# Expert rows one at a time instead of in pairs, with other constants in the planner that places them among a two-layer block's matmuls

## The reference

```python
g = jax.nn.softmax(top, axis=-1).astype(xs.dtype)
a = jax.nn.gelu(jnp.einsum('nd,nhjd->nhj', xs, u[eid]), approximate=False)
return jnp.einsum('nhj,nhjd->nd', g * a, v[eid])
```

## Time and profile before

| | us |
|---|---|
| median of 3 runs (lowest, highest) | 3435.36 (3432.03, 3439.66) |
| profiled execution, its own time | 3441.62 |
| span of its trace | 3439.5 |
| TensorE busy, 82% of the span | 2810.3 |
| DVE busy | 1919.4 |
| ScalarE busy | 1111.6 |

### The profile page before, as it was taken

The page is one execution under the profiler, slowest core; times in us unless marked ns, Lnnn a source line. Parts: engine busy times, 40 slices in busy tenths (PEclk is TensorE's granted clock), DMA queues, the critical chain, the costliest instruction groups (busy, mean ns, idle before and its releaser), DMA issues.

```text
span 3439.5 us, 40717 instructions
## 1 busy us (share of the span) xinstructions
PE 2810.3 (82%) x15162; PEld 1750.6 (51%) x15162; DVE 1919.4 (56%) x4582; ACT 1111.6 (32%) x3213; POOL 853.5 (25%) x772
## 2 busy tenths in 40 slices
PE   8999998989888999888775555699999986655555
PEld 6777887655545666564431111278788841211111
DVE  4564764566676556456676766422300256666665
ACT  2232002343574455323533232232310123323222
POOL 0000001234332333223344444200000034444443
PEclk9999999999999999999898776899999987776776
DMA  8264764989998999879999999733144299999998
GB/s 327 99 208 148 289 239 169 369 339 373 373 358 329 417 421 420 336 299 371 404 372 420 415 412 412 308 111 110 57 152 151 73 376 414 411 419 403 411 415 335
DMA packets 151780, 1071.76 MB, mean 312 GB/s; under 512 B 16668, under 2 KB 19356, under 8 KB 23200
## 3 DMA queue, kind: packets, MB, share of 16 engines
q0 software_dynamic: 110592, 805.36, 57.8%
q1 hardware_dynamic: 40992, 263.82, 20.5%
HBM read 1068.06 MB, written 1.05 MB: 311 GB/s over the span
## 4 chain that ended last, share of the span: by engine, by line
PE 51%; DMA 26%; DVE 12%; ACT 6%; issue 3%; POOL 2%; SPq 0%; DVEq 0%; POOLq 0%; ACTq 0%
PE bank L438 38%; DMA ring<-in_experts,eid 25%; PE bank L452 11%; DVE ring L1494 5%; POOL ring L1968 2%; ACT topk_work L1007 1%; ACT topk_work L1000 1%; DMA ring<-in_quads 1%; ACT topk_work L997 1%; ACT L997 1%; DVE state L1729 1%; PE bank L465 1%; PE bank L687 0%; DVE topk_work L1464 0%; PE bank L568 0%
## 5 line engine op out<-in xcount | busy, mean ns | idle before, releaser
L1968 POOL DMA_INDIRECT ring<-in_experts,eid x768 | 853.3, 1111 | 2563.2 <-PE bank L452 1284.2
L452 PE MATMUL bank<-ring,topk_work 64*64 64x512 f32 x6144 | 975.0, 763 | 557.6 <-ACT topk_work L1007 544.3
L1494 DVE CUSTOM_DVE_ANT_0 ring<-ring,h2tok 128x1024 f32<-128x1024 f32 x768 | 937.4, 1225 | 589.1 <-DMA ring<-in_experts,eid 574.9
L452 PEld LDWEIGHTS bank<-ring,topk_work 64*64 64x64 f32 x6144 | 234.7, 158 | 1185.5 <-ACT topk_work L1007 878.3
L997 ACT ACTIVATE topk_work<-topk_work 128x2 f32<-128x2 f32 x384 | 78.0, 203 | 1139.9 <-DVE topk_work L1494 1132.6
L438 PE MATMUL bank<-h_even,weights 128*128 128x256 f32 (+1 forms) x1280 | 293.2, 388 | 4.4 <-ACT h_even L1080 4.0
L438 PEld LDWEIGHTS bank<-h_even,weights 128*128 128x128 f32 (+1 forms) x1280 | 240.9, 190 | 60.8 <-issue 22.8
L438 PE MATMUL bank<-h_odd,weights 128*128 128x256 f32 (+1 forms) x1008 | 228.3, 382 | 0.0
L1007 ACT ACTIVATE topk_work<-const,topk_work 128x64 f32<-128x64 f32 x768 | 225.6, 341 | 0.2 <-ACT topk_work L1000 0.2
L438 PEld LDWEIGHTS bank<-h_odd,weights 128*128 128x128 f32 (+1 forms) x1008 | 187.5, 189 | 49.9 <-issue 23.8
L1000 ACT ACTIVATE topk_work<-topk_work 128x1 f32<-128x1 f32 x768 | 184.6, 287 | 12.6
(11 more groups left out here) (252 smaller groups left out, 3243.6 us busy)
## 6 DMA issues: line engine op xcount, KB each, us to landing
weights<-in_quads SPq DMA_DIRECT2D x151, 1024.0 KB
ring<-in_quads SPq DMA_DIRECT2D x84, 1024.0 KB, 4.9
ring<-in_experts,eid POOLq DMA_INDIRECT x768
weights<-in_quads SPq DMA_DIRECT2D x6, 768.0 KB
ring<-in_quads SPq DMA_DIRECT2D x6, 768.0 KB, 4.5
weights<-in_quads SPq DMA_DIRECT2D x12, 256.0 KB
xT<-in_xT SPq DMA_DIRECT2D x2, 1024.0 KB, 11.7
out<-state SPq DMA_DIRECT2D x4, 256.0 KB, 5.3
```

The source lines that it names most:

```text
L452: x = nc.tensor.matmul(acc[g][out, :], diag[mine, J % 4, :], ring[mine, J % RING, D + h * 512:D + (h + 1) * 512], start=first, stop=J % TI ...
L1494: v.tensor_tensor_reduce(row, row, h2tok[:, u // UNITS % 2, :], 1.0, 0.0, ALU.mult, ALU.add, dots[:, u % 2, j:j + 1]).then_inc(S["dot_done ...
L1968: pool.indirect_dma_start(ring[:, J % RING, :], None, d["experts"], bass.IndirectOffsetOnAxis(eid[:, u % 2, j:j + 1], 0)).then_inc(gathere ...
```

## The change

Pairs become single rows on TensorE, ScalarE and DVE; counters and marks that counted pairs count rows. ScalarE has a Gelu of one column for each row, 384 more instructions in all. In the planner LAG falls from 5.0 to 4.0, and modelled time is added after each unit of the softmax attention (UNIT_TAKES 2.0), after each of the two gate blocks (GATES_TAKE 5.0) and after the turn of a tile's sums (SUM_TAKES 2.0); `breathe` with a hole looks half of it ahead as before.

```diff
@@ -52,22 +52,22 @@
 UNITS = PH
 TILE_ROWS = UNITS * PTOP
 GROUP_ROWS = 2 * TILE_ROWS
-GROUP_PAIRS = GROUP_ROWS // 2
-TILE_PAIRS = TILE_ROWS // 2
-UNIT_PAIRS = PTOP // 2
 RING = 6
 BANKS = 6
 FIXED, EXTRA = 3, 4
 
 
-PER_LOAD, LANDS, LAG = 2.5, 2.0, 5.0
+PER_LOAD, LANDS, LAG = 2.5, 2.0, 4.0
 LEAD_CHOICE = 10.0
+
+
+UNIT_TAKES, GATES_TAKE, SUM_TAKES = 2.0, 5.0, 2.0
 
 
 BESIDE, PACE = 0.1, 1.0
 DIAG_LAG = 3.0
 
-TURN_FROM, TURN_EVERY, TURN_LAG = 24, 4, 2
+TURN_FROM, TURN_EVERY, TURN_LAG = 48, 8, 4
 
 
 class Count:
...
@@ -437,22 +437,22 @@
                 plan.now += size * 4 / 2400.0
                 return nc.tensor.matmul(out, lhsT, rhs, start=first, stop=last, **kw)
 
-            def row_pair(n):
-                for J in (2 * n, 2 * n + 1):
-                    k, first = J // TILE_ROWS, J % TILE_ROWS == 0
-                    if first and J:
-                        for g in range(2):
-                            pe.wait_ge(*at("evicted", "acc", k - 1, g))
-
-                    pe.wait_ge(S["diag_ready"], J + 1)
-                    for h in range(2):
-                        out = slice(h * BLK, (h + 1) * BLK)
-                        for g in range(2):
-                            mine = slice(g * BLK, (g + 1) * BLK)
-                            x = nc.tensor.matmul(acc[g][out, :], diag[mine, J % 4, :],
-                                                 ring[mine, J % RING, D + h * 512:D + (h + 1) * 512],
-                                                 start=first, stop=J % TILE_ROWS == TILE_ROWS - 1, skip_group_check=True)
-                    x.then_inc(S["row_used"], 1)
+            def row(J):
+
+                k, first = J // TILE_ROWS, J % TILE_ROWS == 0
+                if first and J:
+                    for g in range(2):
+                        pe.wait_ge(*at("evicted", "acc", k - 1, g))
+
+                pe.wait_ge(S["diag_ready"], J + 1)
+                for h in range(2):
+                    out = slice(h * BLK, (h + 1) * BLK)
+                    for g in range(2):
+                        mine = slice(g * BLK, (g + 1) * BLK)
+                        x = nc.tensor.matmul(acc[g][out, :], diag[mine, J % 4, :],
+                                             ring[mine, J % RING, D + h * 512:D + (h + 1) * 512],
+                                             start=first, stop=J % TILE_ROWS == TILE_ROWS - 1, skip_group_check=True)
+                x.then_inc(S["row_used"], 1)
 
             def tile_sum(k):
 
@@ -465,22 +465,22 @@
                             x = nc.tensor.matmul(b[:, c * P + h * BLK:c * P + (h + 1) * BLK],
                                                  sums(k, h)[:, c * P:(c + 1) * P], ident[:, g * BLK:(g + 1) * BLK],
                                                  start=True, stop=True)
+                    plan.now += SUM_TAKES
                     full(x, "yt", k, g)
 
-            def emit(n):
-                landing = plan.row(2 * n + 1)
-                placed_now[n] = (len(job_log), landing)
-                plan.now = max(plan.now, landing + LAG) + 0.2
-                row_pair(n)
-                if n % TILE_PAIRS == 1 and n // TILE_PAIRS in (1, 2, 3):
-                    tile_sum(n // TILE_PAIRS - 1)
-                if n == 5 * TILE_PAIRS + 3:
+            def emit(J):
+                landing = plan.row(J)
+                placed_now[J] = (len(job_log), landing)
+                plan.now = max(plan.now, landing + LAG) + 0.1
+                row(J)
+                if J % TILE_ROWS == 3 and J // TILE_ROWS in (1, 2, 3):
+                    tile_sum(J // TILE_ROWS - 1)
+                if J == 5 * TILE_ROWS + 7:
                     token_sums(0)
-                for J in (2 * n, 2 * n + 1):
-                    plan.now += 0.95
-                    if (J + RING) // GROUP_ROWS == J // GROUP_ROWS:
-                        plan.gather()
-                cur["next"] = n + 1
+                plan.now += 0.95
+                if (J + RING) // GROUP_ROWS == J // GROUP_ROWS:
+                    plan.gather()
+                cur["next"] = J + 1
...
@@ -491,8 +491,8 @@
 
             def breathe(hole=0.0):
 
-                end = plan.now + hole
-                while cur["next"] < cur["limit"] and plan.row(2 * cur["next"] + 1) + LAG <= plan.now + hole / 2:
+                end, early = plan.now + hole, plan.now + hole / 2
+                while cur["next"] < cur["limit"] and plan.row(cur["next"]) + LAG <= max(plan.now, early):
                     emit(cur["next"])
                 plan.now = max(plan.now, end)
 
@@ -709,7 +709,7 @@
                         turn(m)
                     if m and m % 2 == 0:
                         weigh(m // 2 - 1)
-                    breathe()
+                    breathe(UNIT_TAKES)
 
             two = [(0, 0, P), (1, P, P)]
 
@@ -725,7 +725,7 @@
                         b = job("z", n, dd, t)
                         x = mm(b[:, :], ranks[:, tokl(t)], w[:, dd, :], True, True)
                         full(x, "z", n, dd, t)
-                    breathe()
+                    breathe(GATES_TAKE)
 
             def mixer(p):
                 n, i, s = p.n, p.i, p.s
...
@@ -979,34 +979,30 @@
         def _(act):
             cur = {"next": 0, "limit": 0}
 
-            def row_pair(n):
-                J = 2 * n
+            def row(J):
                 u, j = divmod(J, PTOP)
                 par = u % 2
-                if n % TILE_PAIRS == 0 and n // TILE_PAIRS in (1, 2, 3):
-                    tile_out(n // TILE_PAIRS - 1)
-                if n == 5 * TILE_PAIRS + 2:
+                if J % TILE_ROWS == 0 and J // TILE_ROWS in (1, 2, 3):
+                    tile_out(J // TILE_ROWS - 1)
+                if J == 5 * TILE_ROWS + 4:
                     last_squares(0)
-                if n == 5 * TILE_PAIRS + 6:
+                if J == 5 * TILE_ROWS + 12:
                     last_root(0)
                 if j == 0:
                     act.wait_ge(S["wts_ready"], u + 1)
-                m = n % 4 * 2
-
-                act.wait_ge(S["dot_done"], J + 2)
-                nc.scalar.activation(gel[:, m:m + 2], dots[:, par, j:j + 2], ACT.Gelu).then_inc(S["act_gelu"], 1)
-                act.wait_ge(S["act_gelu"], 3 * n + 1)
-                for c in range(2):
-                    nc.scalar.activation(gelw[:, m + c:m + c + 1], gel[:, m + c:m + c + 1], ACT.Copy,
-                                         scale=wts[:, par, j + c:j + c + 1]).then_inc(S["act_gelu"], 1)
+                m = J % 8
+
+                act.wait_ge(S["dot_done"], J + 1)
+                nc.scalar.activation(gel[:, m:m + 1], dots[:, par, j:j + 1], ACT.Gelu).then_inc(S["act_gelu"], 1)
+                act.wait_ge(S["act_gelu"], 2 * J + 1)
+                nc.scalar.activation(gelw[:, m:m + 1], gel[:, m:m + 1], ACT.Copy, scale=wts[:, par, j:j + 1]).then_inc(
+                    S["act_gelu"], 1)
                 if J >= 4:
 
-                    act.wait_ge(S["row_used"], J - 2)
-                for c in range(2):
-                    act.wait_ge(S["act_gelu"], 3 * n + 2 + c)
-                    nc.scalar.activation(diag[:, (J + c) % 4, :], ident_blk, ACT.Copy,
-                                         scale=gelw[:, m + c:m + c + 1]).then_inc(S["diag_ready"], 1)
-                if j == 4 and u + 1 < GROUPS * 2 * UNITS and (u + 1) not in LEADS:
+                    act.wait_ge(S["row_used"], J - 3)
+                act.wait_ge(S["act_gelu"], 2 * J + 2)
+                nc.scalar.activation(diag[:, J % 4, :], ident_blk, ACT.Copy, scale=gelw[:, m:m + 1]).then_inc(S["diag_ready"], 1)
+                if j == 5 and u + 1 < GROUPS * 2 * UNITS and (u + 1) not in LEADS:
                     softmax_exp(u + 1)
 
...
@@ -1035,14 +1031,14 @@
             def rows_until(n):
                 while cur["next"] < n:
                     cur["next"] += 1
-                    row_pair(cur["next"] - 1)
+                    row(cur["next"] - 1)
 
             def rows_before(*key):
 
                 now, when = job_no.get(key, 0), full_at.get(key, 0.0)
                 while cur["next"] < cur["limit"] and cur["next"] in placed:
                     n = cur["next"]
-                    if placed[n][0] > now and not (placed[n][1] + DIAG_LAG <= when and reached(n, now, 2)):
+                    if placed[n][0] > now and not (placed[n][1] + DIAG_LAG <= when and reached(n, now, 4)):
                         break
                     rows_until(n + 1)
...
@@ -1481,29 +1477,28 @@
                 for part in range(16):
                     choose(u, part)
 
-            def row_pair(n):
-                for J in (2 * n, 2 * n + 1):
-                    u, j = divmod(J, PTOP)
-                    if j == 0:
-                        for m in range(2):
-                            if u % UNITS == 0:
-                                dve.wait_ge(*at("evicted", "ht", u // UNITS // 2, u // UNITS % 2, m))
-
-                    dve.wait_ge(gathered[J % RING], 16 * (J // RING + 1))
```

(38 more changed lines are left out.)

26 lines of the change are left out of this document (13 added, 13 removed).

## The result

The changed kernel takes 3473.68 us (median of 4 runs, 3467.75 to 3474.44) beside 3437.51 (4 runs, 3432.03 to 3443.59) of the kernel before on the same chip: ratio 1.0101, 95% interval 1.008 to 1.0122, so 1.0% slower. The forecast was 3421, with a range of 3397 to 3445.

What follows compares the result with a forecast made beforehand. DMA was taken as at full rate in the merge and with rows alone, leaving about 101 us of idle DMA up to 1862 us. Terms -5 - 3 + 6 + 10 + 2.5 - 19 - 6 = -14.5 gave 3421 us, range 3397 to 3445.

Steps and rivals of the forecast that it cites:

- Rows alone: Stretches with only expert rows: slots freed sooner let DMA fill holes where the ring ran dry; -5 us, ends 0 and 20.
- Last rows of a group: Ends of groups 1 and 2: the first of the last two rows is done when the last arrives; 3 us saved.
- More rows earlier in pass 1: 580 to 967 us, ahead of the attention: ten more rows fill DMA and TensorE idle time; +6 us, ends -3 and +20.
- a hole of 31: Idle DMA time from 580 to 967 us, where ten added rows bring 25 us of transfers.
- Attention: Pass 1, 967 to 1083 us, paced by ScalarE: split pairs, more rows and table loads cost +10 us, ends 3 and 17.
- Merge and end of pass 1: Merge: one more row at full rate, +2.5 us; end: 18 fewer rows and an earlier turn of h2, -19 us.
- Pass 2: Twelve more rows before its last projections, so fewer alone afterwards; -6 us net, ends +5 and -14.
- the signs that I had named: DMA shares above 0.95 and 0.9, diagonal waits about 15 us shorter; wrong if attention grows by more than 17 us.
- ScalarE becomes the bound: Rival: split pairs put ScalarE on the path up to and in the attention of pass 1; 3447 us, chance 0.20.
- The rule named in the prediction: Grouping operations helps a saturated engine, splitting one that isn't; so attention pays the whole 17 us, rows alone gain.

Runs made afterwards that it cites:

- e5: Kernel before, with only ScalarE handling each pair as two single rows, TensorE and VectorE places and planner unchanged; 3423.87 us, 0.9942.
- e14: Changed kernel, constants included, but TensorE takes rows in twos while VectorE and ScalarE take them singly; 3436.04 us, 0.9979.
- e17: e14 with at most two rows after a unit of an attention; 3429.57 us, 0.9963.
- e7: Changed kernel with LAG 6.0 and no added times for attention, gates and sums; 3428.48 us, 0.9959.
- e9: Kernel before with single rows on ScalarE only and the new planner constants; TensorE and VectorE keep pairs; 3431.0 us, 0.9971.
- e2: Kernel before, pairs throughout, with the new planner constants (LAG 4.0 and all added times); 3467.18 us, 1.0082.
- e15: e14 with LAG 5 and no added times, TensorE's order nearly that of the kernel before; 3425.71 us, 0.9954.
- e8: e1 with rows in the attention only after every second unit; 3450.52 us, 1.0023.
- e1: Changed kernel with the old planner constants (LAG 5.0, no added times); 3439.24 us, 0.9991.
- e13: Changed kernel, constants included, with at most two rows after each unit of an attention; 3447.99 us, 1.0012.
- e3: Changed kernel with UNIT_TAKES 0 instead of 2.0 and nothing else; 3479.0 us, 1.011.
- e16: e1 with at most two rows after a unit of an attention; 3432.88 us, 0.9971.
- e12: Changed kernel with LAG 5.0 and only the gates' added time of 5.0 kept; 3443.44 us, 1.001.
- e4: Changed kernel with LAG 5.0 instead of 4.0 and nothing else; 3454.99 us, 1.0043.
- e6: Changed kernel with the attention's rows placed between the next scores and the turn of the probabilities; 3471.03 us, 1.0078.

## Why the prediction was wrong

*Rows alone: right, a little small.* Predicted -5; alone fell by 6.6, and dot products 528 to 752 take 565.9 us for 574.2. The rate rose from 412 to 419 GB/s at a share that was 1.01 before as well, so a share of 1.01 did not say that nothing could be won. e5 has all of it without the change of places.

*Last rows of a group: right.* 1.98 us for 3.69.

*More rows earlier in pass 1: the first step that failed.* Predicted +6 (ends -3 and +20), measured +27.9. I counted "25 us of DMA into a hole of 31" and ten rows of TensorE time into 38 idle us. The hole was not filled: the share went from .93 to .94 while the stretch grew. TensorE's idle time was not filled either (42 us, from 38): its wait on diagonals rose from 35.5 to 41.3 us instead of falling with the shorter hold, and its busy time rose by 21.8 us, twice what ten rows are. That second term was not in my sum. With places in twos (e14, to 979 us) the busy time is 360.5 us and the wait 30.7 us, and 16.4 of the 27.9 us come back, with two rows fewer. So single places, with those two rows, are the larger part of the loss; why they cost TensorE busy time no run shows, the granted clock being .95 in all three. What is left, 11.5 to 13.2 us by e14 and e17, goes with eight more rows and the takes. How much of the hole a row can use is open. Among the kernels with single places, 109 rows take 430.0 us (e7) and 118 take 452.5, 2.5 each, a row's whole transfer; from e5 to e9 and from before to e2, six more rows at 46 places cost 22.5 and 23.2 us, 3.8 each; but from e15 to e14 eight cost 11.7, 1.5 each, so there part of the hole was filled. Nor did a run part the number of single places from the two rows that go with it.

*Attention: the second, and the dearer.* Predicted +10 (ends 3 and 17), measured +37.2. The price was summed over ScalarE's instructions: seven for split pairs, five for more rows, five for table loads. e5 splits every pair and its attention takes 3.6 us more, so the 7 was high; e8 has six table loads fewer than e1 and is slower. What I left out was named in the section on the change: units with four and more rows. In such a unit TensorE's one order holds rows whose diagonals aren't there ahead of the next scores and turn, and the engines of the softmax chain stand still in turn. Bounding the heap gives 31.2 of the 37.2 back (e13), with six rows fewer in the stretch (28 for 34), and the end of the pass takes 55.0 us for 46.3; the bound takes 13.5 off e14, with four rows fewer (e17). The count of rows alone doesn't do it: e3 has 31 and takes 126.3 us, e9 has 32 and takes 100.3. Where VectorE takes rows singly the attention goes with the largest heap: 92 to 104 us with two (e13, e15, e16, e17), 105 to 109 with three (e1, e7, e12), 113 to 115 with four (e8, e14), and 119 to 133 with six (e3, e4 and the changed kernel). With pairs on VectorE heaps of four cost nothing that can be seen (e2, e9). e6 shows that moving the heap within the unit doesn't help. A second term that the sum had at nothing is TensorE's clock: from e9 to the changed kernel 33 us lie, and at e9's 0.172 us a matmul the 489 of the changed kernel would be busy 84 us for 95, so about 11 of the 33 are an estimate of what the lower clock costs; most of the rest is waits, 29.4 and 6.9 us for 16.6. What makes the unevenness and VectorE's single rows dear only together is open.

*Merge and end of pass 1: right.* Merge +0.5 for +2.5, end -23.1 for -19 (ends -10 and -24). The turn of h2 waits 4.02 us for the shifts where 7.13 and a pair stood.

*Pass 2: right in sign.* Group 1 with its rows alone -2.6; predicted were -6 and a part of the -5, so the size is less than half of what I said.

*Sum.* Of the signs that I had named, the attention's growth by more than 17 us says "wrong", and the DMA shares above 0.95 and 0.9 and the shorter waits didn't come. -14.5 was predicted; the six stages sum to +33.3 (27.9 + 37.2 + 0.5 - 23.1 - 2.6 - 6.6), of which the two failed steps are 65.1 where 16 stood. The rival "ScalarE becomes the bound" had the direction and the threshold (it decides above 30.5 us in 580 to 1083, and it was 65), but not the mechanism: with TensorE's places unchanged, ScalarE's single rows are a gain of 0.6% (e5), and e9, with new constants, still gains. In ratios, from before to after: single handling -0.46% (e15), new constants +0.25% (e14 less e15, within their intervals), single places with these constants +1.2% (after less e14, clear of them). The last is small with the old constants (e1 less e15, +0.37%), so the loss needs both halves of the change: in e1's attention no heap is larger than three. e2, pairs throughout with the new constants, lost 0.82% where e9 loses nothing; that a late pair, which ScalarE must hold for its second row, is what these constants can't afford is my reading, and no run tests it.

The rule named in the prediction, "Perfetto Trace Analysis", "Optimizing Scalar/DVE Operations" of the Trainium skill, says that breaking instructions up may help when an engine isn't saturated and still makes others wait. e5 agrees, by 0.58%: ahead of the attention, in group 1 and alone it gains. In the attention, where ScalarE was the busier, it cost 3.6 us of the 17 that I had read from the rule.

The best version run is e5 (0.9942): single rows on ScalarE, places as they were. The intervals of e15 (0.9954), e7 (0.9959) and e17 (0.9963) overlap its own.

## What to carry to other kernels

Don't count a hole in a resource as free room for work placed ahead: ask what makes the hole, and whether an added item goes through the same loop (slot, compute, release). Here the added rows cost between 1.5 and 3.8 us each beside other work, where I had counted them as nearly free. When a planner decides places, look at the spread of the heap sizes and not at the totals alone: uneven heaps in the order of an engine that feeds a short chain cost more here than all the instructions that the change added, and a bound of two won nearly all of it back. Change handling and placement apart: here the first was worth 0.5% and was buried by the second.

## What the hardware showed that I had not expected

With rows alone the DMA share read 1.01 at 412 GB/s and again at 419 and 420 GB/s, when the slots came back earlier; the share is no proof of the full rate. And in the worst unit TensorE's clock was low: 24 matmuls took 5.39 us where 8 take 1.09 in the rows around them (24 would be 3.3), after it had waited 2.81 us, and the granted clock from 1060 to 1066 us is .50, the lower of its two levels. Behind the wait of 6.91 us two rows took 3.69 us where two take 1.95. The granted clock is .86 over the changed kernel's attention, .89 in e13 and .95 in e9, at 489, 443 and 474 matmuls; e9 was shown above:

```profile
993.00:1126.00 133.00, 95.24 (x489) 45.27 (x488) 80.46 (x216) 87.24 (x181) 34.69 (x33) 0.86 0.74 270
```
